# A hybrid encoder layer on one core: four orders of work changed at the start, before the experts and at the end

## What is computed

```python
zq, zf, zi, zg, fq, fk, fv, ff = split_projection(x @ p['w_in'])
y = concatenate([hgrn2_readout(o, zg, p['hg_g']), fox(q, k, v, logf)], axis=-1) @ p['w_out']
x = layer_norm(DN_ALPHA * x + mix, p['ln1_g'], p['ln1_b'])
x = layer_norm(DN_ALPHA * x + memory_attend(x, mk, mv, p['xa_wq'], p['xa_wo']), ...)
return layer_norm(DN_ALPHA * x + hier_moe(x, p), p['ln3_g'], p['ln3_b'])

# hier_moe: a group of 4, then the two best of its 8 experts, for each row
g_sel = argmax(x @ w_group + b_group)
top_v, top_i = top_k((x @ w_expert + b_expert)[g_sel], 2)
gate = softmax(top_v) * softmax(group logits)[g_sel]
y[row] = sum over its two experts of gate * (silu(x @ w_gate[e]) * (x @ w_up[e])) @ w_down[e]
```

## Time and profile before

| | us |
|---|---|
| median of three runs | 1826.71 (1825.23 to 1828.67) |
| the profiled execution | 1822.11 |
| its span, first to last instruction | 1820.3 |
| TensorE busy in it | 1628.2 (89%) |
| VectorE busy | 715.6 (39%) |
| ScalarE busy | 338.2 (19%) |
| GpSimd busy | 173.7 (10%) |

### The profile page before, as it was taken

One profiled execution on the slowest core, in us unless ns is written; L12 is line 12 of the kernel. 1 busy time (PEld: TensorE's weight loads), 2 busy tenths in 40 slices (PEclk: granted clock), 3 DMA queues, 4 the chain that ended last, 5 costly groups with the idle time before them and its releaser, 6 DMA issues. The chain is left out here.

```text
span 1820.3 us, 30717 instructions
## 1 busy us (share of the span) xinstructions
PE 1628.2 (89%) x13557; PEld 1003.0 (55%) x13557; DVE 715.6 (39%) x1153; ACT 338.2 (19%) x764; POOL 173.7 (10%) x191
## 2 busy tenths in 40 slices
PE   8989999999999998999998999948999888879940
PEld 4555456666664555445666666635656555556520
DVE  1212457735453354234002433374343333333228
ACT  2332236511001243011001111100110000000115
POOL 0000000000101231000100000003111111111026
PEclk9999999989999999999999999958999999989975
DMA  6171003011101232414011001185999999999985
GB/s 215 47 256 48 1 7 135 2 47 46 58 1 46 67 121 98 161 35 153 1 46 46 24 12 70 70 338 207 421 421 420 422 421 420 423 420 423 423 311 192
DMA packets 71597, 321.93 MB, mean 177 GB/s; under 512 B 13177, under 2 KB 25465, under 8 KB 58913
## 3 DMA queue, kind: packets, MB, share of 16 engines
q1 hardware_dynamic: 49488, 278.69, 38.4%
q10 hardware_dynamic: 15248, 20.46, 3.5%
q0 software_dynamic: 6720, 20.72, 3.1%
HBM read 283.72 MB, written 36.11 MB: 176 GB/s over the span
## 5 line engine op out<-in xcount | busy, mean ns | idle before, releaser
L926 PE MATMUL psum<-arena 128*32 128x256 f32 x5376 | 314.9, 395 | 52.9 <-DMA arena<-in_moe_w_up 47.3
L926 PEld LDWEIGHTS psum<-arena 128*32 128x32 f32 x5376 | 198.3, 114 | 166.8 <-issue 78.8
L485 PE MATMUL psum<-arena 128*128 128x512 f32 x528 | 231.8, 597 | 3.9 <-DMA arena<-in_w_in 3.9
L470 PE MATMUL psum<-arena 128*128 128x352 f32 x768 | 229.9, 462 | 0.0
L1549 DVE COPY arena<-psum 128x512 f32<-128x512 f32 (+6 forms) x132 | 82.9, 634 | 361.5 <-PE psum L485 162.9
L470 PEld LDWEIGHTS psum<-arena 128*128 128x128 f32 x768 | 147.0, 192 | 82.5 <-issue 2.4
L485 PEld LDWEIGHTS psum<-arena 128*128 128x128 f32 x528 | 99.8, 192 | 123.7 <-issue 123.2
L1249 ACT ACTIVATE arena<-psum 128x128 f32<-128x128 f32 (+7 forms) x196 | 93.0, 476 | 352.8 <-PE psum L463 294.1
L940 PE MATMUL psum<-arena 128*32 128x256 f32 x2688 | 151.8, 379 | 4.0 <-issue 3.3
L2176 POOL DMA_INDIRECT arena<-x_rows,consts x84 | 79.8, 950 | 713.3 <-DVE arena L1982 351.0
L463 PE MATMUL psum<-consts,arena 128*128 128x128 f32 (+5 forms) x783 | 119.0, 284 | 16.4 <-ACT arena L1249 6.9
(11 more groups left out here) (288 smaller groups left out, 1564.2 us busy)
## 6 DMA issues: line engine op xcount, KB each, us to landing
arena<-in_moe_w_gate SPq DMA_DIRECT2D x32, 2048.0 KB, 31.6
arena<-in_moe_w_down SPq DMA_DIRECT2D x32, 2048.0 KB, 38.8
arena<-in_moe_w_up SPq DMA_DIRECT2D x32, 2048.0 KB, 36.7
arena<-in_w_in SPq DMA_DIRECT2D x7, 2048.0 KB, 8.7
y_blocks<-arena ACTq DMA_DIRECT2D x1, 9216.0 KB, 50.5
y_blocks<-arena ACTq DMA_DIRECT2D x64, 96.0 KB, 23.5
arena<-in_x_prompt SPq DMA_DIRECT2D x9, 512.0 KB, 3.6
y_blocks<-arena ACTq DMA_DIRECT2D x72, 64.0 KB, 26.0
```

The costliest lines, as they stand in the source:

```text
L470: last = mm(ps[:, c * BANK:c * BANK + THIRD], lhs(k), rhs[:, k, c * THIRD:(c + 1) * THIRD], start=(k == 0), stop=(k == KD - 1))
L485: last = mm(ps[0:n, c * 512:(c + 1) * 512], lhs(k), rhs(k)[:, c * 512:(c + 1) * 512], start=(k == 0), stop=(k == KD - 1))
L926: last = mm(out, xeT[:, b, a, k, :], w[:, :, k, j * P:(j + 1) * P], start=(k == 0), stop=(k == KD - 1))
```

## The change

Four places are written anew.

1. The key weights are loaded as two transfers, four of the eight steps of k each; tile 0's matmuls wait for the first half (`fk_half`) and, ahead of step 4, for the second.
2. Tile 8's keys are transposed into banks 6 and 7 and copied by ScalarE ahead of the zero transfer and the gates' functions. The two tiles of cache keys are transposed, in the same banks, behind query groups 0 and 1, and copied behind the copies of these groups.
3. `choose` runs for tiles 0 to 4 and 5 to 8 instead of 0 to 5 and 6 to 8. The first call moves from step 9 to step 8.
4. The second gather of a tile adds to `g1` by the transfer itself (`compute_op`), after a wait for the tile's first gather. GpSimd issues three tiles' first gathers ahead. The additions on VectorE and GpSimd and the tensor `g2` are gone. The residual comes back in three transfers, each with its own semaphore.

```diff
@@ start, TensorE
-                w = weights(pe, "fk")
-                rows(("FK", t), [2 + t % 2], "dve", lambda k: xT[:, k, cols_of(t)], lambda k: w[:, k, :], n)
+                w = wslot[0]
+                if t == 0:
+                    pe.wait_ge(fk_half, 16)
+                def fk_rows(k):
+                    if t == 0 and k == 4:
+                        weights(pe, "fk")
+                    return w[:, k, :]
+                rows(("FK", t), [2 + t % 2], "dve", lambda k: xT[:, k, cols_of(t)], fk_rows, n)
...
-                turn_keys(("KT", NT - 1, j), [j], fk[:, NT - 1], DEC, j)
+                turn_keys(("KT", NT - 1, j), [6 + j], fk[:, NT - 1], DEC, j)
...
-            for t in range(2):
-                for j in range(2):
-                    turn_keys(("KC", t, j), [2 + j], kc_in[:, t], P, j)
...
                 columns(("FQ", m), [[0, 1, 2], [3, 4, 5]][m % 2], "act", lambda k: w[:, k, m * P:(m + 1) * P], xT)
+                if m < 2:
+                    for j in range(2):
+                        turn_keys(("KC", m, j), [6 + j], kc_in[:, m], P, j)
@@ start, SP
-                sp.dma_start(wslot[0], w_p[:, :, off["fk"]:off["fk"] + 512]).then_inc(w_loaded[0], 16)
+                sp.dma_start(wslot[0][:, 0:4], w_p[:, 0:4, off["fk"]:off["fk"] + 512]).then_inc(fk_half, 16)
+                sp.dma_start(wslot[0][:, 4:8], w_p[:, 4:8, off["fk"]:off["fk"] + 512]).then_inc(w_loaded[0], 16)
@@ start, ScalarE
+            for j in range(2):
+                turned_keys(("KT", NT - 1, j), ka, SEQ, DEC, j)
             act.wait_ge(zeros_ready, 1)
             act.dma_start(y_dram[UNITS * 32:UNITS * 32 + NOVER * C, :].rearrange("(j p) n -> p j n", p=C),
...
-            for j in range(2):
-                turned_keys(("KT", NT - 1, j), ka, SEQ, DEC, j)
-            for t in range(2):
-                for j in range(2):
-                    turned_keys(("KC", t, j), kac, t * P, P, j)
...
                 take(last, ("FQ", m))
+                if m < 2:
+                    for j in range(2):
+                        turned_keys(("KC", m, j), kac, m * P, P, j)
@@ choice of experts, VectorE
-                    for t0, t1 in ((0, 6), (6, NT)):
+                    for t0, t1 in ((0, 5), (5, NT)):
@@ closing stage, SP
-            sp.dma_start(x1[:, 0:NT - 1, :], x2_dram[0:SEQ, :].rearrange("(t p) n -> p t n", p=P)).then_inc(x2_back, 16)
-            sp.dma_start(x1[0:DEC, NT - 1, :], x2_dram[SEQ:T, :]).then_inc(x2_back, 16)
+            for i in range(2):
+                sp.dma_start(x1[:, 4 * i:4 * i + 4, :],
+                             x2_dram[4 * i * P:4 * (i + 1) * P, :].rearrange("(t p) n -> p t n", p=P)).then_inc(x2_back[i], 16)
+            sp.dma_start(x1[0:DEC, NT - 1, :], x2_dram[SEQ:T, :]).then_inc(x2_back[2], 16)
@@ closing stage, VectorE
-                    if s in PAIRS_DVE:
-                        dve.wait_ge(g_in[s], 32)
-                        link(TT(g, g, g2[0:n, s, :], ALU.add))
-                    else:
-                        dve.wait_ge(pair_ready, PAIRS_POOL.index(s) + 1)
+                    dve.wait_ge(x2_back[s // 4], 16)
+                    dve.wait_ge(g_in[s], 32)
                     STT(y, y, ALPHA, g, ALU.mult, ALU.add).then_inc(sum_ready, 1)
@@ closing stage, GpSimd
+            def pair_row(t, k):
+                if k == 1:
+                    pool.wait_ge(g_in[t], 16)
                 n = rows_of(t)
-                pool.wait_ge(g_in[t], 32)
-                Q.tensor_tensor(g1[0:n, t, :], g1[0:n, t, :], g2[0:n, t, :], ALU.add).then_inc(pair_ready, 1)
...
+                pool.indirect_dma_start(out=g1[0:n, t, :], out_offset=None, in_=y_dram,
+                                        compute_op=ALU.add if k else ALU.bypass,
+                                        in_offset=bass.IndirectOffsetOnAxis(ap=dest_i[0:n, k, t:t + 1], axis=0))\
+                    .then_inc(g_in[t], 16)
+            AHEAD = 3
+            for t in range(NT + AHEAD):
+                if t < NT:
+                    pair_row(t, 0)
+                if t >= AHEAD:
+                    pair_row(t - AHEAD, 1)
```

More of the change, by code:

```diff
@@ L257, in build @@
         g1 = view(0, "t n", t=NT, n=D)
-        g2 = view(NT * D, "t n", t=NT, n=D)
         scrap = at(R + 9216, D)
-        PAIRS_DVE = (0, 1, 3)
-        PAIRS_POOL = [t for t in range(NT) if t not in PAIRS_DVE]
         psum = ctx.enter_context(nc.psum_tensor("psum", [P, 8 * BANK], F32))
@@ L273, in build @@
         w_loaded = [sem(f"w_loaded{i}") for i in range(2)]
-        par_loaded = sem("par_loaded")
+        par_loaded, fk_half = sem("par_loaded"), sem("fk_half")
         cache_loaded = sem("cache_loaded")
@@ L303, in build @@
         x2_stored = [sem(f"x2_stored{i}") for i in range(2)]
-        x2_back = sem("x2_back")
+        x2_back = [sem(f"x2_back{i}") for i in range(3)]
         xe0_in = [sem(f"xe0_in{i}") for i in range(NS)]
@@ L319, in build @@
         g_in = [sem(f"g_in{i}") for i in range(NT)]
-        sum_ready, pair_ready = sem("sum_ready"), sem("pair_ready")
+        sum_ready = sem("sum_ready")
         fin_ready, mean_ready, centered = sem("fin_ready"), sem("mean_ready"), sem("centered")
@@ L2041, in _ @@
             dve.wait_ge(ln3_loaded, 32)
-            dve.wait_ge(x2_back, 32)
             for s in range(NT + 2):
@@ L2201, in _ @@
             pool.wait_ge(fin_ready, 1)
-            def pair_sum(t):
+            def pair_row(t, k):
+                if k == 1:
+                    pool.wait_ge(g_in[t], 16)
                 n = rows_of(t)
-                pool.wait_ge(g_in[t], 32)
-                Q.tensor_tensor(g1[0:n, t, :], g1[0:n, t, :], g2[0:n, t, :], ALU.add).then_inc(pair_ready, 1)
-            for t in range(NT):
-                n = rows_of(t)
-                for k, g in enumerate((g1, g2)):
-                    pool.indirect_dma_start(out=g[0:n, t, :], out_offset=None, in_=y_dram,
-                                            in_offset=bass.IndirectOffsetOnAxis(ap=dest_i[0:n, k, t:t + 1], axis=0))\
-                        .then_inc(g_in[t], 16)
-                if t - 2 in PAIRS_POOL:
-                    pair_sum(t - 2)
-            for t in range(NT - 2, NT):
-                if t in PAIRS_POOL:
-                    pair_sum(t)
+                pool.indirect_dma_start(out=g1[0:n, t, :], out_offset=None, in_=y_dram,
[8 more added lines that the diff above has]
+                    pair_row(t - AHEAD, 1)
 _INS = ["x_prompt", "x_sample", "cache_fox_k", "cache_fox_v", "cache_fox_logf", "state_hgrn", "cache_mem_k",
```

## The result

The changed kernel takes 1799.7 us (median of four runs, 1799.11 to 1801.68), the kernel before, timed beside it, 1826.78 (1825.23 to 1828.67): 27.1 us less. The ratio is 0.9849, with a 95% interval of 0.9831 to 0.9866. The profiled execution took 1799.99 us around a span of 1798.2.

A forecast was written before the change was run, and what follows sets the result against it. TensorE was taken to bound the time up to the experts, weight transfers among them. Gains of 2.5 + 7.7 + 5.8 + 8.2 = 24.2 us off the 1826.7 median gave 1802.5; the 8-in-10 range was 1795 to 1812.

The forecast's parts named there:

- Part 1: Start: with key weights in halves the first key matmul starts near 7.8 us; 2.5 us won, bounds 1.3 and 3.1.
- the two ways of the slow first tile: Tile 0's half-rate time either moves with the work (2.9 us won) or ends at the same moment (1.4 won).
- Part 2: Before the query projection: cache keys' transposes move behind two query groups; net 7.7 us, bounds 7.2 and 8.3.
- rival (c): At the start: fill and decay store last until today's 156, swallowing the first two gains; 1812.7 us, chance 0.06.
- Part 3: Router: the five-tile choice fits VectorE's idle time and tile 8's sum comes sooner; net 5.8 us, bounds 5.3 and 8.5.
- The plus of 2.7: Router's tile 7: with the wait down to about 2 us TensorE may stay at full clock, worth another 2.7 us.
- Part 4: Closing stage: second gathers add by transfer, leaving VectorE three operations a tile; 8.2 us won, range 2 to 11.5.
- The plain-cost case: Closing stage: an accumulating gather costs what a plain one does, so the last tile starts 10.4 us sooner.
- The low bound of 2: Closing stage: if GpSimd needed 0.6 us more per accumulating issue, a tile would cost 5 us and 2 be won.
- (a): Closing stage: accumulating gathers pace the end at one per 5.2 us, its gain is nothing; 1810.7 us, chance 0.14.
- (b): Closing stage: accumulating gathers run one at a time, 8.0 us each, 4.3 us slower; 1831.0 us, chance 0.05.
- (d): Start: both key weight halves interleave and land together near 10.7, winning nothing there; 1805.0 us, chance 0.05.

The follow-up runs named there:

- part 4 alone: Kernel before, with each tile's second gather adding by transfer, pair sums on VectorE and GpSimd gone, residual in three transfers; 1817.99 us.
- five ahead: Changed kernel with five first gathers issued ahead instead of three, all second gathers still adding; 1800.55 us, ratio 0.9865.
- half rows: Changed kernel whose adding gathers move and add only 512 of 1024 columns, from another place in the table; 1795.54 us in a single execution.
- two tiles apart: Changed kernel with tiles 0 and 1 gathered plain into two buffers and added on VectorE; 1798.87 us, ratio 0.9854.

## Why the prediction was right, and where it wasn't

The time came out 2.8 us below the forecast of 1802.5 and inside its range, with none of the rivals' times. But two terms missed by some 2 us in opposite directions, so part of the closeness is luck.

**Part 1** (2.5 forecast): 2.78 in the profile, 2.6 in the median alone. TensorE started at 7.51, not 7.8, because the first half was there before ScalarE's copy; the second half was in time, as worked out. Of the two ways of the slow first tile, the one in which the slow time moves with the work held: that tile took 9.49 us, after 9.09. It is itself drawn, 8.64 to 10.11 in five executions of the old start and 8.69 to 10.13 in nine of the new.

**Part 2** (7.7, bounds 7.2 to 8.3): mis-sized, too small, and its bounds too narrow. Between the two first profiles it is 8.69, by medians 10.0. From the second tile's transposes to the query projection it won 10.03 where 9.70 were counted. The sixteen transposes took 1.75 us from one query group to the next (0.87 and 0.88), not 2.01. The rest is the clock at the seam, which the sum had in its bounds alone, with half a microsecond: the old queries started at half clock after the wait, and how long they stayed there is drawn. The first 10 us of the query projection in before, in part 4 alone (whose start is before's) and after, with the granted clock third from the end:

```profile
99.34:109.34 10.00, 10.00 (x34) 6.48 (x34) 3.54 (x4) 1.06 (x2) 0.00 (x0) 0.97 1.03 356
```
```profile
98.68:108.68 10.00, 10.00 (x28) 6.30 (x28) 3.55 (x4) 1.06 (x2) 0.00 (x0) 0.80 1.03 356
```
```profile
86.53:96.53 10.00, 10.00 (x36) 6.48 (x35) 6.47 (x12) 3.10 (x7) 0.00 (x0) 1.00 1.02 357
```

From the second tile's transposes to the values the five executions with the old order take 136.9 to 138.6 us, the nine with the new one 128.2 to 128.3: part 2 is worth 8.7 to 10.4 us, 9.4 in the mean. The prediction worked from one execution, and that one was the quickest of the five. The cover was as named: no wait on banks 6 and 7, and rival (c), the decay store, did not come.

**Part 3** (5.8): 5.9 in the profiles (185.0 to 179.1). Tile 8's sum met its matmuls, and the clock fell, as taken. The plus of 2.7 that was left as a bound does exist: in the kernel with five ahead, whose choice is the changed kernel's, the router's tile 7 took 2.40 us behind the same wait, at a mean granted clock of 0.79 instead of 0.50, and the stage took 176.3 us instead of 179.1:

```profile
1182.06 2.40 PE L860 MATMUL psum<-consts,arena 128*128 128x36 f32 x16 [2.21 <-ACT arena L1256]
```

It came in one of nine profiled executions with this choice.

**Part 4** (8.2, range 2 to 11.5): 6.3 between the first profiles, 6.6 by the means of the stage (60.0 to 53.4). Two steps failed. The first sum was put at 12.3 us and came at 13.8: the 7.34 us of flight were a plain gather's. With plain second gathers in the same order it came at 12.48, so 1.3 us are the addition's. And even with the doubled load, which the sum took, the last three tiles were to go at VectorE's own pace of 3.53 us; it waited for gathers to tile 7, and a tile took 3.77 on average. Not counted were the output rows, which SP stores tile by tile over the same sixteen engines. From 1774 to 1784, while VectorE waited for gathers at tiles 5 and 6 (0.48 and 0.25 us), the stores took more than a third of the engines' time:

```profile
q0 software_dynamic: 377, 1.33, 66.5%
q1 hardware_dynamic: 392, 1.45, 38.2%
```

How much of the delay is theirs was not measured apart. The load of the gathers was a fair guess: 4.0 us a tile forecast, 4.2 measured (34.7 us for eight tiles and a quarter). The plain-cost case, a gain of 10.4 or a last sum at 39.6 us, was right for plain gathers: 39.12. The low bound of 2 had as its condition that an adding issue takes GpSimd 0.6 us more. It does (1.55 for 0.94), but a tile did not cost 5 us: with half rows the issues were as long, up to 2.03 beside VectorE's work, and VectorE kept its own pace.

By the Trainium skill, Collectives: The Full Stack, section "The bandwidth ceiling: the fold count and why AG ≠ RS ≠ AR", the add in a ReduceScatter's transfers makes them slow for its two source reads. The runs agree for a gather that adds: it costs 1.9 plain ones.

**Rivals.** (a) came true as a mechanism, the adding gathers pace, at 3.8 us instead of 5.2, near enough to VectorE's own pace to cost 2 us and no more. The prediction's sign for it, waits beyond tile 3, was there, and the last sum came 30.2 us after the first, just past the 27 to 30 named. (b): landings overlap, 11.99 us of flight beside issues 2.4 to 2.8 us apart. (d): the halves landed apart; the first matmul ran at 7.51.

**Taking span gains off the median** gave 1802.5; taken off the profiled execution they would have given 1797.9. The truth lay between, since before's execution was a quick draw and after's was not. By the means of the stages the gain is 13.1 + 6.0 + 6.6 = 25.7, with nothing clear of the noise among the experts, and the medians of all runs (1825.9 of 44 for before, 1799.7 of 8 for after) say 26.2.

## What to carry to other kernels

Read a gain of a few microseconds stage by stage from several executions: here the stages behind the router repeat within 1.3 us (but for one quick execution), while the first half varies by 5, enough to fake a loss in a part that has none. An add in a gather frees two engines but costs the DMA engines 1.9 plain gathers; where transfers and the consuming engine are near balance, let the idle consumer add the first pairs itself and keep enough plain gathers ahead that the queue never runs dry. And count all traffic of a stage, the stores of its results too, before saying which engine paces it.

## What the hardware showed that was not expected

- The same code draws half-clock stretches of different length from execution to execution: some 17 or 24 us at the attention's end (granted clock 0.72 or 0.60 over 30 us), and 0.97 to 0.80 over the first 10 us of the old query projection. After the same wait of 2.21 us the router's tile 7 took 3.62 or 3.63 us in eight executions and 2.40 in one.
- An adding gather's issue takes GpSimd 1.55 to 1.61 us, a plain one's 0.94, also with half as many bytes; beside VectorE's work up to 2.27 in the changed kernel and 2.60 with two tiles apart.
- The DMA engines read as full (share 1.03 to 1.07) at 256 to 295 GB/s with adding gathers in the mix, where plain gathers and stores moved 394 at 1.00.
